# Diagonal 64-token blocks for masked reads in the delta-rule units of a two-layer kernel

## What is computed

```
def step(S, inp):                       # per head; S is 64 x 64
    r_t, w_t, k_t, v_t, kk_t, a_t = inp
    sa = jnp.einsum('bhvk,bhk->bhv', S, -kk_t)
    S = (S * w_t[:, :, None, :] + sa[..., None] * (kk_t * a_t)[:, :, None, :]
         + v_t[..., None] * k_t[:, :, None, :])
    y = jnp.einsum('bhvk,bhk->bhv', S, r_t)
...
y = ((y - mu) * lax.rsqrt(var + RWKV_GN_EPS))            # over each head's 64 values
y = y * rwkv_ln_w + rwkv_ln_b
rwkv_out = (y + bonus) * jax.nn.silu(rg)
o = o * lax.rsqrt(mean(o * o) + NORM_EPS) * gla_norm_w
gla_out = o * jax.nn.silu(gg)
merged = jnp.concatenate([gla_out, rwkv_out], axis=-1)
return x + merged @ w_out
```

## Time and profile before

| | |
|---|---|
| three runs | 2272.12, 2276.91, 2282.65 us |
| the profiled execution | 2272.56 us, span 2270.8 us |
| TensorE busy | 2169.0 us (96%) |
| VectorE, ScalarE, GpSimd busy | 1566.1, 993.7, 607.3 us |
| mean granted TensorE clock | 0.986 |
| unit loop, first turn -1 to the output product | 2006.65 to 2172.49 us |
| output product and final norm | 2172.49 to 2270.8 us |

### The profile page before, as it was taken

The page is one execution under the profiler, slowest core; times in us unless marked ns, Lnnn a source line. Parts: engine busy times, 40 slices in busy tenths (PEclk is TensorE's granted clock), DMA queues, the critical chain, the costliest instruction groups (busy, mean ns, idle before and its releaser), DMA issues. The chain is left out here.

```text
span 2270.8 us, 44030 instructions
## 1 busy us (share of the span) xinstructions
PE 2169.0 (96%) x18388; PEld 1377.1 (61%) x18388; DVE 1566.1 (69%) x2009; ACT 993.7 (44%) x1731; POOL 607.3 (27%) x379
## 2 busy tenths in 40 slices
PE   7999989999999899899999999999999999989998
PEld 4666665556666566566666665448644445568747
DVE  7876887988888755787777774247787575236654
ACT  3226765666666543524444443235553332224321
POOL 3555673100000220073333331000154532101160
PEclk9999999999999899999999999999999999999999
DMA  3113213677777622111111113326424532033412
GB/s 133 47 55 89 87 64 73 131 142 136 144 144 145 134 107 78 44 56 42 56 57 57 57 52 118 99 73 207 133 87 135 160 101 86 18 98 99 167 61 75
DMA packets 287948, 218.33 MB, mean 96 GB/s; under 512 B 203328, under 2 KB 253696, under 8 KB 286352
## 3 DMA queue, kind: packets, MB, share of 16 engines
q1 hardware_dynamic: 287760, 215.64, 35.0%
HBM read 145.77 MB, written 25.76 MB: 76 GB/s over the span
## 5 line engine op out<-in xcount | busy, mean ns | idle before, releaser
L1499 DVE TENSOR_TENSOR_SCAN att_left<-att_left,att_unseen_prefix 16x16 f32<-16x16 f32 (+5 forms) x144 | 177.3, 1271 | 16.4 <-ACT att_left L1327 16.1
L2888 PE MATMUL ps<-second_x_hi,whi_z 128*128 128x512 f16 (+1 forms) x480 | 178.8, 372 | 3.4 <-POOL wlo_z L2857 1.9
L1221 PE MATMUL ps<-x_hi,whi_z 128*128 128x348 f16 x560 | 176.0, 314 | 4.4 <-DVE att_q L1431 4.4
L2889 PE MATMUL ps<-second_x_lo,whi_z 128*128 128x512 f16 (+1 forms) x480 | 178.5, 372 | 0.0
L2890 PE MATMUL ps<-second_x_hi,wlo_z 128*128 128x512 f16 (+1 forms) x480 | 178.5, 372 | 0.0
L1223 PE MATMUL ps<-x_hi,wlo_z 128*128 128x348 f16 x560 | 174.9, 312 | 0.0
L1222 PE MATMUL ps<-x_lo,whi_z 128*128 128x348 f16 x560 | 174.9, 312 | 0.0
L1341 ACT ACTIVATE att_left_split<-att_left 128x256 f16<-128x256 f32 (+7 forms) x128 | 87.3, 682 | 141.7 <-DVE att_left L1499 127.7
L2189 PE MATMUL ps<-x_lo,whi_z 128*128 128x342 f16 x432 | 133.2, 308 | 0.0
L2188 PE MATMUL ps<-x_hi,whi_z 128*128 128x342 f16 x432 | 132.9, 308 | 0.0
L2190 PE MATMUL ps<-x_hi,wlo_z 128*128 128x342 f16 x432 | 132.6, 307 | 0.0
(11 more groups left out here) (655 smaller groups left out, 6256.2 us busy)
## 6 DMA issues: line engine op xcount, KB each, us to landing
wraw_z<-in_w_second SPq DMA_DIRECT2D x30, 512.0 KB, 4.1
wraw_z<-in_w_up SPq DMA_DIRECT2D x26, 512.0 KB, 3.7
wraw_z<-in_w_qkv SPq DMA_DIRECT2D x24, 512.0 KB, 4.4
wraw_z<-in_w_down SPq DMA_DIRECT2D x20, 512.0 KB, 3.6
raw_down<-in_w_down SPq DMA_DIRECT2D x20, 512.0 KB, 4.2
seg<-dt_a_sums SPq DMA_DIRECT2D x18, 512.0 KB, 5.3
wraw_z<-in_w_up SPq DMA_DIRECT2D x36, 256.0 KB, 3.3
second_work<-parked_units SPq DMA_DIRECT2D x7, 1280.0 KB, 6.1
```

The source lines that it names most:

```text
L1221: nc.tensor.matmul(lin_ps(g), hi, xhi, start=(kb == 0), stop=False)
L1499: nc.vector.tensor_tensor_scan(x, x, unseen, 1.0, ALU.mult, ALU.max).then_inc(s_scan, 1)
L2888: nc.tensor.matmul(out, hi, xhi, start=(j == 0), stop=False)
L2889: nc.tensor.matmul(out, hi, xlo, start=False, stop=False)
```

## The change

**Reads.** `wide_products` becomes `own_products`: 16 matmuls of 64 x 64 per call in place of 8 of 64 x 128, two per head, and no off-diagonal square is made. `rb` and `rk` keep 64 columns per head, and the two masks on VectorE take 512 in place of 1024 columns. `read_values`, the second half of `removal_maps` and the former last group of `values` (now `read_removed`) each become 16 matmuls with 64 output columns that contract over one block's 64 tokens.

**Banks.** The two blocks of a unit's outputs now lie in banks 6 and 7, with `y` in the left and the read maps in the right halves of both. The sums of `means` and `variances` go to banks 0 and 2 (bank 7 for the last unit), the transposed keys to banks 1 and 2, the key values to bank 0. The waits that guard the banks change with them. `means` moves ahead of `read_removed`.

**Gate products.** The product of a unit with its gate (units 0 to 6) and of a head with its gate go from VectorE to GpSimd, ahead of the low parts in its loop. The last unit's gate product stays on VectorE.

**High parts.** ScalarE writes the high parts behind the copies of L3863 and L3867 of the same turn, no longer ahead of them.

```
@@ unit phase, views
-        rb = part(flat, 4 * SEQ, 2 * SEQ).rearrange("p (s h n) -> p s h n", s=2, h=H)
-        rk = part(flat, 6 * SEQ, SEQ).rearrange("p (h n) -> p h n", h=H)
+        rb = part(flat, 4 * SEQ, SEQ).rearrange("p (s h n) -> p s h n", s=2, h=H)
+        rk = part(flat, 5 * SEQ, SEQ // 2).rearrange("p (h n) -> p h n", h=H)
...
-        y_ps, rr_ps = bank(6), bank(7)
+        y_ps, rr_ps = (S.ps[:, 6:8, o * RWKV_P * SUB:(o + 1) * RWKV_P * SUB].rearrange("p k (q n) -> p k q n", n=SUB) for o in range(2))
+        mean_ps, var_ps = (lambda c, b=b: bank(7 if c == NUNIT - 1 else b) for b in (0, 2))
@@ GpSimd, for c in range(1, NUNIT + 1)
-                    if 2 <= c < 2 + GLA_HEADS:
-                        h = c - 2
-                        pool.wait_ge(s_ghi, h + 1)
-                        nc.gpsimd.tensor_tensor(mlo[:, h, :], o[:, h, :], mhi[:, h, :], ALU.subtract).then_inc(s_glo, 1)
+                    if c < NUNIT:
+                        yc, at = y[:, (c - 1) % 2, :, :], slice((c - 1) * P, c * P)
+                        pool.wait_ge(s_v, FSTEPS * c - 1)
+                        nc.gpsimd.tensor_tensor(yc, yc, gate[:, :, at], ALU.mult).then_inc(s_v, 1)
+                    if c <= GLA_HEADS:
+                        pool.wait_ge(s_gv, 2 * c - 1)
+                        nc.gpsimd.tensor_tensor(o[:, c - 1, :], o[:, c - 1, :], og[:, c - 1, :], ALU.mult).then_inc(s_gv, 1)
                     if c == NUNIT - 1:
                         cut_first(nc, S, pool, L)
...
                     nc.gpsimd.tensor_tensor(mlo[:, RWKV_P:2 * RWKV_P, (c - 1) * P:c * P], y[:, (c - 1) % 2, :, :],
                                             mhi[:, RWKV_P:2 * RWKV_P, (c - 1) * P:c * P], ALU.subtract).then_inc(s_lo, 1)
+                    if c <= GLA_HEADS:
+                        pool.wait_ge(s_ghi, c)
+                        nc.gpsimd.tensor_tensor(mlo[:, c - 1, :], o[:, c - 1, :], mhi[:, c - 1, :], ALU.subtract).then_inc(s_glo, 1)
@@ TensorE
-                def wide_products(c, key, kind, out):
-                    for h in ORDER:
-                        last = nc.tensor.matmul(out[:, h * P:(h + 1) * P], held(c)[half(h), key, h % RWKV_P, :], held(c)[half(h), kind, h % RWKV_P, :],
-                                                start=True, stop=True)
+                def own_products(c, key, kind, out):
+                    for k, h in kh:
+                        last = nc.tensor.matmul(out[sub(k), h // RWKV_P, h % RWKV_P, :], held(c)[half(h), key, h % RWKV_P, sub(k)],
+                                                held(c)[half(h), kind, h % RWKV_P, sub(k)], start=True, stop=True)
...
-                    for h in ORDER:
-                        nc.tensor.matmul(y_ps[half(h), y_cols(h)], tkv[:, c % 2, 1, h % RWKV_P, h // RWKV_P, :], rk[:, h, :], start=first(h), stop=False)
+                    for k, h in kh:
+                        nc.tensor.matmul(y_ps[half(h), k, h % RWKV_P, :], tkv[sub(k), c % 2, 1, h % RWKV_P, h // RWKV_P, :], rk[sub(k), h, :],
+                                         start=first(h), stop=False, skip_group_check=True)
...
                     pe.wait_ge(s_y, c + 1)
-                    pe.wait_ge(s_rrc, min(c + 2, NUNIT))
+                    if c + 2 < NUNIT:
+                        pe.wait_ge(s_rkm, c + 3)
...
@@ VectorE
                     for q in range(RWKV_P):
                         last = nc.vector.scalar_tensor_tensor(yc[:, q, :], yc[:, q, :], col(S, "rwkv_ln_b_2", q), bc[:, q, :], ALU.add, ALU.add)
+                    if c < NUNIT - 1:
+                        last.then_inc(s_v, 1)
+                        return
                     step(last)
...
-                    dve.wait_ge(s_gv, 2 * h + 1)
-                    nc.vector.tensor_tensor(o[:, h, :], o[:, h, :], og[:, h, :], ALU.mult).then_inc(s_gv, 1)
```

86 lines of the change are left out of this document (52 added, 34 removed).

## The result

The changed kernel takes 2281.97 us (median of 20 executions, 2274.95 to 2296.42) beside 2276.67 of the kernel before; the ratio is 1.0029, interval 1.0017 to 1.0040. It is 0.3% slower, where 0.7% faster was forecast. Three executions far above the others of their kernel (one each of e5, e16 and e17, at 2458.89, 3167.5 and 7759.14 us) are left out of the ratios. The profiled execution of the changed kernel has a span of 2282.9 us against 2270.8.

The account below looks back on a forecast made before the run. TensorE, busy 96% of the span, was taken as the bound. Loop -20.2, gate product +5.5, clock +0.3 sum to -14.4 us: 2258.2 from the profiled 2272.56, 2262.5 in the median's frame, stated as 2260; range 2249 to 2276.

Parts of the forecast that it names:

- the sum of the loop: Unit loop up to T7, the start of turn 7: all gains there together, 20.2 us.
- rival C: Unit loop: TensorE instructions arrive too slowly; at 49 per us 28 us more, 2288 us; chance 0.13.
- Products and readers: Two product calls and three readers a turn run on four quadrants in about half the time: 2.55 us a turn.
- D: Rival: the new groups run on two quadrants only, 0.6 in place of 2.55 us a turn, 2274 us; chance 0.07.
- ScalarE's wait: Before a turn's transposes, TensorE waits for ScalarE's copy: 0.65 us stays where 0.73 was; turn 1 newly gets it.
- A: Rival: GpSimd's gate product holds VectorE off the shared port, 0.7 us in turns 2 to 5, 2263 us; chance 0.09.
- Masks, small edits: VectorE's masks halve, gaining 1.1 us once in turn -1; bank waits and low parts of heads cost 0.
- The gate product of unit 6: On GpSimd ahead of cut_first, it delays the output: block 3 starts 5.5 us later, TensorE idles 6.5 us.
- The clock: At the output's start, the 6.5 us idle drops TensorE's clock: cost 0 to 1.5 us, 0.3 taken.
- Turns 5 and 6: Place beside the weight loads where late instruction supply was to show first.
- B: Rival: fewer changes of shape save 2.8 us, an absent ScalarE wait makes it 5.4; 2255 to 2257 us; chance 0.13.

Follow-up runs that it names:

- e5: Kernel before with only the two read products on 64-token blocks, readers, banks, masks and engines untouched: 2273.63 us, ratio 0.9993.
- e16: e12 with the 4 MB load of parked_h issued in turn 7 and not in turn 5: 2262.95 us, ratio 0.9944.
- e17: Kernel before with only the 4 MB load of parked_h issued in turn 7 and not in turn 5: 2273.54 us, ratio 0.9990.
- the second profiles: Both kernels profiled once more, unchanged: loop start to start of turn 7 took 155.13 us in the kernel before, 149.04 in the changed one.
- m1: TensorE alone, no kernel: stretches of 64x64 matmuls, 64x128 matmuls, then 64x64 beside loads; 256 instructions come every 3.73 us in the first, 6.2 in the third.
- e2: Kernel before with only the gate products on GpSimd and the high parts behind ScalarE's copies, reads 128 wide: 2278.38 us, ratio 1.0012.
- e10: Kernel before with readers on 64-token blocks, products wide, gate products and high parts left in place: 2275.23 us, ratio 0.9992.
- e3: Changed kernel with cut_first ahead of the gate product of unit 6 on GpSimd: 2275.42 us, ratio 0.9999.
- e13: e3 with both read products wide again and the 4 MB load of parked_h issued in turn 7, not turn 5: 2264.89 us, ratio 0.9938.
- e12: e3 with the read products wide again, except the keys' product on 64-token blocks in units 1 to 7: 2267.07 us, ratio 0.9954.
- e11: e3 with both read products on 64-token blocks in units 1 to 7, wide only in the prologue: 2276.12 us, ratio 0.9993.
- e4: Kernel before, its five wide groups issued as twice as many 64-column matmuls, neighbours of the products sharing an array half: ratio 1.0086.
- e7: Kernel before, its five wide groups issued as twice as many 64-column matmuls, neighbours alternating between array halves: ratio 1.0092.
- e9: e3 with 19 full matmuls that nobody reads put ahead of four waits of the prologue: 2279.61 us, ratio 1.0018.

## Why the prediction was wrong

**The step that failed** is the sum of the loop, -20.2 us before T7: it puts gaps of instruction supply at nothing. Measured, the loop became 6.1 us shorter in the second profiles and 6.5 us longer in the first, with 17.6 and 20.0 us of gaps without a releaser where the kernel before has 3.7 and 2.9. The reason for the nothing was rival C's own test: "It decides from below 54 per us", with 60.5 needed, and "Against: 128 records passed in 1.09 us in L3511". An average rate does not decide. m1 shows 256 instructions per 3.73 us, 69 per us, so on average the supply would have done even for the changed kernel (1035 records in 17.1 us). But it comes block by block: the changed kernel put its fast groups side by side (L3597, L3521 and L3514 are 256 instructions in 2.1 us), and what follows such a block waits up to 1.6 us. Slack in slow blocks is not banked (m1's third stretch, behind its slow second one). And 1.09 us for L3511 shows only what happens inside a block that has arrived. The signs were in the trace: in the earlier trace rows a gap without a releaser leaves 14 of a group's 16 records behind it, and the next such gap, 0.52 us in turn 6, stands 127 records on. I put the first down to the loads and did not count. Rival C, given 0.13, was the right mechanism at a smaller price (11.3 us net, not 28). The 49 per us in its price is in no row; in m1 the supply was 69 per us without loads and 41 beside them.

**Products and readers**, 2.55 us a turn: the shape was right (0.5 us a group, four quadrants; D is dead). Net of gaps, turns 0 to 6 fell by 1.9 to 2.55 us in the second profiles, 2.13 in the mean; the term was some 20% too large.

**ScalarE's wait**: 0.65 us was to stay in turns 1 to 4. In turn 4 the transposes start at T+3.88, as forecast (T+3.95), but the supply gap of 0.54 us stands in the wait's place; in e2, which has the moves and no new short groups, the wait is gone altogether. What the moves are worth beside short readers e10 shows: 7.2 us of waits in turns 2 to 5. A did not happen: VectorE's L3790 (L3759 before) takes 1.28 us as before.

**Masks, small edits**: the changed kernel's turns 0 to 6 have no new wait for a bank or a mask over 0.2 us; price 0 as forecast. The 1.1 us once in turn -1 can't be told from the clock there.

**The gate product of unit 6**: forecast +5.5 at block 3, measured 6.0 and 6.55, and 6.5 us in time by e3. TensorE idles 6.57 us where 6.5 was written. Right, and the clearest single part. (In its chain 11.3 + 1.15 is 12.45 and not 12.6, which changes nothing.)

**The clock**: 0.3 us was forecast, for the idle at the output's start. There it was about right: block 0 lasts 2.3 us longer than before, and block 3 still waits 0.46 us for its cut. The prologue was not thought of: with products on blocks or split, it has 14 to 20 us more at half clock in six of seven profiles. The price of that in time stays open between 0 and some 5 us.

**Turns 5 and 6**, named as C's first place, were that: 9.2 and 7.5 us of gaps in two profiles where the kernel before has 3.4 and 3.8. That the load is the cause is shown by e13 for turn 6, with short readers and wide products; the changed kernel itself was not run with the load moved.

**The range.** Its lower end is a slip: B's two terms (5.4 us) under the 2258.2 of the profiled execution's frame give 2252.8, not 2249. The measured 2281.97 lies above its upper end, 2276.

## What to carry to other kernels

Before making instructions smaller, count them. Where 256 TensorE instructions in a row (here 64 matmuls of float32) would run in less than about 3.7 us, the next block is not there, and the saving ends at that floor. Judge it block by block and not by the mean; a slow group among fast ones can cost nothing (e12 against e11). Keep large loads away from such stretches. When a group gets shorter, ask again what its engine will then wait for (e10), and when an instruction is moved to an in-order engine, look at what stands behind it (e3).

## What was not expected of the hardware

- In m1 a block of 256 TensorE instructions (16 KB) came every 3.73 us without loads and every 6.2 us beside 408 GB/s of them, though its matmuls need 2.09 us without loads, and the slack of slow blocks was not stored.
- With 64x128 weights, halving the columns from 128 to 64 changed 68 ns an instruction to 60 (e4, e7). In m1 128 columns took 56 ns (7.15 us for 128 records), and the weight loads were busy for all 42.41 us of that stretch, so it is probably they that set the time.
- Two executions of one kernel had 27.3 and 3.4 us of half clock at the same place, 6 us apart in turn -1 alone (20.18 and 13.91).
- More work in the waits (e9) shortened the half clock there to 3.4 us and did not shorten the kernel.
